# Hybrid decoder layer on one core: 112 identity products on TensorE ahead of the gate stage

## What is computed

```python
h = x + mix(rms_norm(x))                       # conv module and gated MLP, one output projection
h = h + hierarchical_moe(rms_norm(h))          # 16 experts, 2 per token
gate = sigmoid(rms_norm(h) @ w_ple_gate)       # 1024 x 1024
h = h + (p @ w_ple_proj) * gate
y = rms_norm(h)
```

## Time and profile before

| | |
|---|---|
| median of three runs | 643.48 us (642.16 to 644.73) |
| the profiled execution's own time | 645.81 us |
| its span, first to last instruction | 644.0 us |
| mean granted TensorE clock | 0.963 |
| PE busy | 591.2 us, 92% of the span, 3442 instructions |
| DVE busy | 511.8 us, 79% |
| ACT busy | 363.1 us, 56% |
| POOL busy | 200.3 us, 31% |

### The profile page before, as it was taken

How to read it: one execution, slowest core, us unless ns; L and a number is a source line. 1 busy time by engine, 2 the same in 40 slices (tenths; PEclk the granted TensorE clock), 3 DMA queues, 4 the chain that set the end, 5 groups by cost and what they waited for, 6 DMA issues and landing times.

```text
span 644.0 us, 9882 instructions
## 1 busy us (share of the span) xinstructions
PE 591.2 (92%) x3442; PEld 508.4 (79%) x3442; DVE 511.8 (79%) x555; ACT 363.1 (56%) x374; POOL 200.3 (31%) x208
## 2 busy tenths in 40 slices
PE   3799999989999888899999999999999999459994
PEld 3799999968787667688888888888888888359993
DVE  4768998996633776789999999999999999397545
ACT  6712222426435627577777787777777777334343
POOL 8063636982000018322212222222221221122004
PEclk9799999989999889999999999999999999869997
DMA  9986111045142336799999999999999999480003
GB/s 257 277 260 240 66 67 66 1 140 183 49 159 89 126 102 223 263 365 391 384 390 383 392 372 376 348 394 375 387 379 371 371 391 344 136 294 3 1 1 147
DMA packets 79065, 153.99 MB, mean 239 GB/s; under 512 B 8411, under 2 KB 26419, under 8 KB 78579
## 3 DMA queue, kind: packets, MB, share of 16 engines
q1 hardware_dynamic: 71627, 138.98, 60.9%
q0 software_dynamic: 5520, 9.56, 4.0%
q10 hardware_dynamic: 1888, 5.05, 2.2%
HBM read 147.90 MB, written 14.41 MB: 252 GB/s over the span
## 4 chain that ended last, share of the span: by engine, by line
PE 77%; DVE 7%; POOL 6%; DMA 3%; issue 3%; SPq 2%; ACT 1%; POOLq 0%; ACTq 0%; DVEq 0%
PE pair L1649 21%; PE pair L1651 20%; PE pair L1650 20%; PE pair L1696 8%; PE pair L1660 3%; POOL slots L765 2%; DMA two<-normed,gidx 2%; DVE lo L1197 1%; SPq L466 1%; PE pair L2004 1%; POOL h L692 1%; POOL h L694 1%; DMA two<-in_state_conv 1%; DMA two<-normed,vecs 1%; POOL lo L609 1%
## 5 line engine op out<-in xcount | busy, mean ns | idle before, releaser
L1649 PE MATMUL pair<-hi,act_hi 128*128 128x512 f32 (+3 forms) x748 | 276.8, 370 | 6.8 <-DVE act_lo L1490 2.6
L1197 DVE TENSOR_TENSOR lo<-raw,hi 128x2048 fp32r<-128x2048 f32 x111 | 251.4, 2290 | 33.6 <-ACT hi L837 33.4
L1651 PE MATMUL pair<-hi,act_lo 128*128 128x512 f32 (+3 forms) x748 | 269.5, 360 | 0.0
L1650 PE MATMUL pair<-lo,act_hi 128*128 128x512 f32 (+3 forms) x748 | 269.3, 360 | 0.0
L837 ACT ACTIVATE hi<-raw 128x2048 fp32r<-128x2048 f32 x119 | 224.9, 1916 | 50.6 <-PE pair L1651 24.6
L1649 PEld LDWEIGHTS pair<-hi,act_hi 128*128 128x128 f32 (+1 forms) x748 | 140.2, 187 | 34.1 <-issue 6.7
L1651 PEld LDWEIGHTS pair<-hi,act_lo 128*128 128x128 f32 (+1 forms) x748 | 139.6, 187 | 22.8 <-issue 0.6
L1650 PEld LDWEIGHTS pair<-lo,act_hi 128*128 128x128 f32 (+1 forms) x748 | 140.2, 187 | 19.5 <-issue 0.4
L748 POOL DMA_INDIRECT pairs<-two,sidx x17 | 43.2, 2539 | 112.8 <-DVE two L1498 112.8
L1243 DVE SCALAR_TENSOR_TENSOR pair<-conv,vecs,pair 128x512 f32<-128x512 f32 x112 | 74.9, 749 | 0.0
L837 ACT ACTIVATE act_hi<-pair 128x1024 fp32r<-128x1024 f32 (+3 forms) x50 | 38.1, 781 | 63.0 <-PE pair L1660 36.7
(11 more groups left out here) (222 smaller groups left out, 505.9 us busy)
## 6 DMA issues: line engine op xcount, KB each, us to landing
raw<-in_w_exp_gate SPq DMA_DIRECT2D x34, 1024.0 KB, 8.5
raw<-in_w_exp_up SPq DMA_DIRECT2D x34, 1024.0 KB, 9.0
raw<-in_w_exp_down SPq DMA_DIRECT2D x34, 1024.0 KB, 10.2
h<-in_x_prompt SPq DMA_DIRECT2D x8, 512.0 KB, 6.3
raw<-in_w_in SPq DMA_DIRECT2D x8, 512.0 KB, 7.4
raw<-in_w_in SPq DMA_DIRECT2D x4, 1024.0 KB, 9.7
raw<-in_w_out SPq DMA_DIRECT2D x4, 1024.0 KB, 7.9
raw<-in_w_ple_gate SPq DMA_DIRECT2D x4, 1024.0 KB, 10.8
```

The costliest lines, as they stand in the source:

```text
L1197: nc.vector.tensor_tensor(lo[:, n % SPLIT, :], raw[:, n % RAW, :], hi[:, n % SPLIT, :].bitcast(F32), ALU.subtract).then_inc(lo_dve, 1)
L1649: mm(out_, x_hi, w_hi, start=start, stop=False)
L1650: mm(out_, x_hi, w_lo, start=False, stop=False)
L1651: return mm(out_, x_lo, w_hi, start=False, stop=stop)
```

## The change

Behind the last `down` of the expert stage, PE multiplies `ident` by itself 112 times, as one accumulation into the first 128 columns of `bank[5]`. Nobody reads the result, and nothing waits for it. The operands are plain float32. No other engine's program changes. Behind the products stand, as before, the wait on `jobs_done`, the register load, the branch and the first wait of the gate stage.

```diff
@@ -87,6 +87,7 @@
 LANE = 32
 LANES = P // LANE
 LOGIT_AT = 256
+KEEP = 112
 MIX, FFN, GATE, FINAL = range(4)
@@ -2042,6 +2043,9 @@
             down(N_GATE - 2, STEPS - 1)


+            for i in range(KEEP):
+                mm(bank[5][:, 0:P], ident[:, :], ident[:, :], start=(i == 0), stop=(i == KEEP - 1))
+
             pe.wait_ge(jobs_done, 1)
             jobs_n = pe.value_load(jobs_i[0:1, 2 * OVERFLOW_MAX:], min_val=0, max_val=OVERFLOW_MAX)
```

## The result

The changed kernel takes 652.27 us in the median of four runs (650.42 to 652.79), against 642.82 us for the kernel before (four runs, 641.09 to 644.73). The ratio is 1.0151 with a 95% interval of 1.0130 to 1.0173, so about 9.7 us are lost, 8.4 to 11.1. The forecast was 653.7 us, 10.2 us over the median shown.

The account below looks back on a forecast made before the run. PE was taken to bound the gate stage. Products of 24.4 us overrun its idle room by 12.3 us, 2.1 come back, and 10.2 us on the 643.48 median gives 653.7 us; range 650.0 to 658.0.

Parts of the forecast that it names:

- The number of passes: Behind the last down product: 112 plain float32 products count double, giving 224 weight loads with 224 passes on PE.
- The length of a pass: In the added products: 0.109 us from start to start, taken from transposes and 80-column passes; 24.4 us in all.
- the stage's move: Gate stage behind the added products: starts later, moving tile 1's transposes from 579.83 to 590.0, by 10.2 us.
- The bounds 0.090 and 0.126: Ends for one pass in us, from full-weight rows of 16 and 32 columns; the stage moves by 6.0 or 14.0 us.
- The overrun and the hand-over: Gate stage's entry: products end at 582.2, 12.3 us past the room's end at 569.84; head product follows at 584.3.
- the mark: Start of tile 1's transposes in the gate stage, showing the stage's position: 579.83 before, predicted 590.0 after.
- The clock: Head of gate stage: never-idle PE keeps 2.4 GHz; twelve head products at 0.12 instead of 0.213 us, 1.1 us back.
- The sequencer: PE's register load and branch behind the products: costed at nothing, up to about 1 us if not run ahead.
- The one in which the products fit: Products end about 569.9, within PE's idle time, leaving only the clock's effect: 642.1 us, about 0.2% change; chance 0.07.
- gave way during the products: Half clock through the added products: 49 us in all, stage moves about 37 us, to 680 us; chance 0.04.
- fell again behind them: Clock falls after PE's idle time from 583.1 to 584.3; slower head products cost 1.4 us, 655.1 us; chance 0.12.
- The page: Trainium skill's contrary price for the added products: 81 ns per load and product, 18.1 us, moving the stage about 4 us.

## Why the prediction was right, point by point

*The number of passes.* 224, as counted from the x2 rows. The runs with one pass per product confirm that this decides: they take 642.63 and 641.56 us where the change takes 652.27.

*The length of a pass.* Taken 0.109 from the transposes, measured 0.1117. The products last 25.0 us instead of 24.4. This 0.6 us is nearly all by which the stage's move was undersized against the same profile: 10.2 predicted, 10.86 measured. The bounds 0.090 and 0.126 were not needed; the 0.090 was read from a single pair of 16 columns, and the stream of such passes had 0.109. The prediction sorted its rows by the size of the weights; with 64 weights in one half a pass cost 0.110 us all the same.

*The overrun and the hand-over.* The stage starts when the passes end. From the head's first transpose to the first product I worked out 2.1 us (582.2 to 584.3); it is 580.46 - 578.36 = 2.10. From that product to the mark 5.8 us were worked out, and it is 5.83. PE did not wait for DVE's row of tile 1.

*The clock.* 1.00 from 550 us on, as forecast, and 1.3 to 2.3 us is its worth in the head, by the run with 50 products against the two profiles of the kernel before. But the reason given, that a PE which is never idle gives no cause for a fall, is not enough: it fell in a stream without gaps when the products had 16 columns.

*The sequencer.* Costed at nothing, up to 1 us at the upper end. The head's transposes follow the last pass without idle time, so it is nothing.

*The rivals.* The one in which the products fit was worked out as 642.1 us, under the condition that a product takes less than 0.107 us. The 50 products, whose stream also fits, took 642.18. The condition did not hold for 112 products, at 0.223 us each. In the profile the clock neither gave way during the products nor fell again behind them; the idle stretch there was 1.07 us, as against 1.2 worked out.

*The page.* The Trainium skill's 81 ns for a load and product of 128 columns ("TensorE: Matmul & The Clock Gate", section "Back-to-back issue gap") would have given a move of about 4 us. No stream of 128 weights here went under 0.109 us, and the measured move is outside of it.

*The total.* 652.27 against 653.7 us. The predicted sum stood on a median of 643.48; that of four runs is 642.82, and this accounts for 0.7 of the 1.4 us. The rest is 10.2 us predicted against 9.45 between the medians. The pass was priced too low, which by itself would have made the sum too small. The position of the head before the change was taken from one profile, in which the mark stood 22.31 us behind D; from the other one, with 23.59, the same working would have given a move of 8.9. The mechanism and its sizes were right, but that the total came within 1.4 us is in part luck: these two errors go opposite ways.

## What to carry to other kernels

Work put into an engine's idle gap is free only up to the moment at which that engine is wanted again, and beyond that it costs its full length. So price it by rows of the same type and shape, and count the instructions: a plain float32 product was two passes, a transpose or an fp32r product one. Where the only aim is to keep TensorE's clock up, know the worth first (here 1.3 to 2.3 us of 643 in the head), fill in two parts, with the second behind a wait on the data that ends the gap, and measure the gap in more than one execution, since its length moved by more than the gain.

## What the runs showed of the hardware that was not expected

- A stream without gaps did not always hold TensorE at 2.4 GHz. With 16 columns per pass the granted clock fell to 0.50 about 4 us into the stream, while the profile shows PE busy; behind 112 fp32r products of 128 columns it fell within 1 us of idle time, and behind 104 transposes it was 0.50 after 2.50 us; behind plain float32 products of 128 columns it was 1.00 after 1.78 us, and behind fp32r products of 256 columns after 0.57 us. Each of these is one execution.
- Float32 transposes held it for 12.4 us.
- A plain float32 pass of 128 columns took 0.110 us with 64 weights in one half of the output partitions and 0.055 us when two halves took turns. With 128 weights and 16 columns it took 0.109 us at full clock and 0.213 us at 0.50.
- The gap on PE had a second author: in the profiles of the 50 products and the 104 transposes, among others, the last result waited for the scatter of the step before, not for PE. PE took up the head's first row between 12.3 us behind D, in the kernel before, and 569.98 - 555.73 = 14.25 us, with the 104 transposes. What makes that scatter take longer in some executions was not examined.
